# Branch merge and output projection computed in high and low parts, with the parts added on GpSimd

## The chip, the cores and the metric

One core of a Trainium2 chip runs the whole program. The metric is the device time of one execution in microseconds (us), the median of several runs. The engines are named as the profile names them: PE (TensorE matmul; PEld is its weight load), DVE (VectorE), ACT (ScalarE), POOL (GpSimd), SP (SyncE, which here issues nearly all transfers).

## What is computed

An encoder of two layers over 768 rows (a prompt of 256, a sample of 512), width 1024, in float32. Per layer four attention branches (A, B, C, X) give outputs `oa`, `ob`, `oc` (512 wide) and `ox` (256 wide); then come the lines that the change touches, and then 16 experts chosen by their top rows:

```python
merged = (gates[:, :, 0] * (oa @ wb[BR_A:BR_B])
          + gates[:, :, 1] * (ob @ wb[BR_B:BR_C])
          + gates[:, :, 2] * (oc @ wb[BR_C:BR_X])
          + gates[:, :, 3] * (ox @ wb[BR_X:]))
x = x + merged @ w_out[l]
x = x + expert_choice_moe(rms_norm(x, norm2_g[l]), w_router[l], w_gate_up[l], w_down[l])
```

## The kernel before

The program is written per engine, each with its instructions in a fixed order, and the engines wait for each other on counted signals (`Signal`; `at(l, k)` is the k-th event of layer l). A layer runs through these stages: norms and projections of the rows, the attention of A, B, C and X, the merge, the output projection with the second norm and the router between its tiles, the choice of rows, and the experts.

Most matrix products are already in three single-pass parts: `product3` (L1782) multiplies high by high, high by low and low by high, all of type float32r, into one bank. ACT makes a high part as a copy with rounding, DVE the low part as the difference of the raw value and the high part. The gate columns of `w_in` are multiplied like this between the attention's matmuls (`gate_part`, L1833 to L1848), and ACT and SP put them into `g_cols` in DRAM.

The merge is different: it multiplies plain float32. PE goes over 8 column tiles `c` of 128, within each over the 4 branches `b`, and within each over two groups of rows (512 and 256); a group is 4 matmuls in depth (2 for X) of the weights `wdir` with the attention outputs `oT` (L2016 to L2029). Four banks turn. DVE multiplies each bank by the gate (L1654, L1657) and, for the last three branches, adds it to `mT` (L1659). ACT takes the sigmoid of the gates `G` (L1178). SP loads `oT` after the last pair of heads, then `wdir` in pieces of 1792 KB, `G` in pieces of 1536 KB, the projection's weights `wout0`, `wout1`, and `X2`, the rows to be added to (L711 to L742). `wdir` lies in the memory of the gate weights, so its first piece waits until all of those are split (`load_branch(0, lo_made, NGEMM - 1)`), behind the last gate stores on the queue.

The output projection (`project`, L2032 to L2043) multiplies `mT` by `wout` in 12 groups of 8 matmuls of 512 columns, with the transposes and router matmuls of the tile before in between (`turn_h`, `route`). DVE adds the residual (L1665), norms, and picks the top rows (L1699 to L1703). Then POOL gathers the first expert's rows, PE transposes them, ACT and DVE split them, and the experts start. The first two pairs of expert weights (`EARLY`, L758) are loaded after the merge, the rest after the projection's last matmul.

Of the kernel before, what the change touches and what calls it, by code (L numbers as in the profile page):

```python
# [12 lines left out]
P = 128  # L13
# [11 lines left out]
NE = 16  # L25
# [23 lines left out]
EARLY = 2  # L49
TILES = (2, 3, 4, 5, 0, 1)  # L50
NSAMPLE = 4
# [128 lines left out]
def build(nc, x_in, mem_in, w, gains, tables, y_prompt, y_sample):  # L180
    ctx = ExitStack()
    with ctx:
# [20 lines left out]
        fgs = sb("fgs", [P, 2, 512])  # L203
        mkv = sb("mkv", [P, MT, 2 * 4 * HD])
# [72 lines left out]
        wdir = take("wdir", [P, 2, 2 * SLOT])  # L277
        wout0 = take("wout0", [P, KD, 512])
# [4 lines left out]
        wkvp = take("wkvp", [P, 2, 4 * HD])  # L283
        take = rows_region()
# [77 lines left out]
        oT = take("oT", [P, 14, NTOK])  # L362
        mT = take("mT", [P, KD, NTOK])
        wout1 = take("wout1", [P, KD, 512])
        gp = take("gp", [P, 2, NTOK])

# [102 lines left out]
        o_in = dma_sig("o_in", 1)  # L469
# [3 lines left out]
        br_in = [dma_sig(f"br_in{i}", 2) for i in range(2)]  # L473
# [4 lines left out]
        wo_in = [dma_sig(f"wo_in{i}", 1) for i in range(2)]  # L478
# [65 lines left out]
        def o_of(br, h, s):  # L544

            t0, nt = SEQS[s]
            r, c = slice(h % 2 * HD, (h % 2 + 1) * HD), slice(t0 * P, (t0 + nt) * P)
            if br.name == "X":
                return oT[r, 12 + h // 2, c]
            return (OSB if br.name in "AC" and h < 2 else OS)[r, c]  # L550
# [32 lines left out]
        def _(sp):  # L583
# [29 lines left out]
            for l in range(DEPTH):  # L613
# [97 lines left out]
                sp.dma_start(oT[:, 0:12, :], o_rows[:, :].rearrange("(k p) n -> p k n", p=P)).then_inc(o_in.sem, 16)  # L711
                for g in (14, 15):
                    for i in range(4):
                        store_gate(l, g, i)

                def load_branch(n, before, k0):

                    sp.wait_ge(before.sem, before.at(l, k0))
                    sp.dma_start(wdir[:, n % 2, 0:14 * CW].rearrange("p (k n) -> p k n", n=CW),
                                 kpn(lay(w["w_branch"], l)[:, :, n * CW:(n + 1) * CW])).then_inc(br_in[n % 2].sem, 16)  # L720

                def load_gates(c):
                    sp.wait_ge(br_ev.sem, br_ev.at(l, 8 * (c - 1) - 1))
                    sp.dma_start(G[:, c % 2], g_cols[:, :].rearrange("(b q p) n -> p b q n", p=P, q=KD)[:, :, c, :])\
                      .then_inc(g_in[c % 2].sem, 16)

                load_branch(0, lo_made, NGEMM - 1)
# [4 lines left out]
                load_branch(1, fg_mm, 4 * NGATE - 1)  # L732
                load_gates(1)
                for c, wo in enumerate((wout0, wout1)):
                    sp.wait_ge(o_ev.sem, o_ev.at(l, 55))
                    sp.dma_start(wo[:], kpn(lay(w["w_out"], l)[:, :, c * 512:(c + 1) * 512])).then_inc(wo_in[c].sem, 16)
# [20 lines left out]

                for i in range(EARLY):  # L758
                    load_pair_m(l * NE, i)
# [31 lines left out]
        def _(pool):  # L791
# [21 lines left out]
            for l in range(DEPTH):  # L813
# [3 lines left out]
                norm_p(l, BR["X"], 0)  # L817

# [48 lines left out]
        def _(act):  # L867
# [133 lines left out]

            def attend(l, br, it, halves):
# [27 lines left out]
                for u, (h, s, t, last) in enumerate(br.units):  # L1030
# [20 lines left out]
                    if br.name == "C" and it == 0 and u == 4:  # L1051
                        cx_roots(l, 3).then_inc(x_root.sem, 1)
                    for g, i in copies.get(u, []):
                        gate_copy(l, g, i)
# [26 lines left out]
            for l in range(DEPTH):  # L1081
# [93 lines left out]
                for c in range(KD):  # L1175
                    act.wait_ge(g_in[c % 2].sem, g_in[c % 2].at(l, c // 2))
                    for b in range(4):
                        act.activation(G[:, c % 2, b, :], G[:, c % 2, b, :], ACT.Sigmoid).then_inc(g_sig.sem, 1)  # L1178
# [31 lines left out]
                for h in range(2):  # L1210
                    part_copies(l, xs_t, h, 7, xsT_hi[:, 4 * h:4 * h + 4, :], xs_hi)
# [53 lines left out]
        def _(dve):  # L1265
# [198 lines left out]

            def attend(l, br, it, quarters):
# [69 lines left out]
                for u, (h, s, t, last) in enumerate(br.units):  # L1535
# [21 lines left out]
                    if br.name == "C" and it == 0:  # L1557
                        x_norm(l, u)
                    if last:
# [11 lines left out]
            for l in range(DEPTH):  # L1571
# [74 lines left out]
                for c in range(KD):  # L1646
                    for b in range(4):
                        dve.wait_ge(g_sig.sem, g_sig.at(l, 4 * c + b))
                        for h, (t0, n) in enumerate(((256, 512), (0, 256))):
                            q = 8 * c + 2 * b + h  # L1650
                            gate, acc = G[:, c % 2, b, t0:t0 + n], mT[:, c, t0:t0 + n]
# [556 lines left out]
```

## Time and profile before

| what | value |
|---|---|
| median of 3 runs | 3387.19 us (3383.3 to 3391.39) |
| the profiled execution | 3385.0 us, span 3383.2 us |
| PE busy | 3148.2 us, 93% of the span |
| DVE, ACT, POOL busy | 2092.1, 1881.2, 348.0 us |
| mean granted TensorE clock | 0.979 of full speed |

The span runs from the first to the last instruction. A line such as L2027 is a line of the kernel printed above. A float32 matmul shows as two records in the profile, a float32r matmul as one. The chain of waits is followed back from the last instruction; what lies on it sets the time.

### The profile page before, as it was taken

To read this page: it belongs to the slowest core of one execution; us is meant where nothing else is said; L and a number is where in the kernel's file an instruction comes from. 1 tells how busy PE (TensorE), PEld (TensorE's weight loads), DVE (VectorE), ACT (ScalarE), POOL (GpSimd) and SP (SyncE) were. 2 spreads that over 40 slices of the span, in tenths; PEclk is the share of its full clock that TensorE was granted. 3 is DMA by queue.
4 is the path that set the end of the run, shared out by engine and by line. 5 is a ranking of instruction groups with operands and counts; after the bars stand their busy time and mean duration, and the time that the engine had idled before them with its cause. 6 is when DMAs were issued, how large, how long until landed. Compare 5 with 4: busy or idle time off the path is not lost.

```text
span 3383.2 us, 45998 instructions
## 1 busy us (share of the span) xinstructions
PE 3148.2 (93%) x16388; PEld 2394.2 (71%) x16388; DVE 2092.1 (62%) x3016; ACT 1881.2 (56%) x3018; POOL 348.0 (10%) x476
## 2 busy tenths in 40 slices
PE   7999989899999799999999899998989988999997
PEld 7978777777555477777698787777765545777775
DVE  4565455664333788888846654556634347888886
ACT  4365555555213577777744755555541136777775
POOL 0021111111000111111000211101110001111110
PEclk9999999999999799999999999999999998999999
DMA  6112111222631799999941121111245237999996
GB/s 222 52 59 68 46 46 44 71 75 89 247 133 62 274 387 384 386 389 381 337 138 49 58 66 48 49 58 61 75 156 210 103 121 282 382 388 387 383 390 247
DMA packets 272987, 626.41 MB, mean 185 GB/s; under 512 B 14784, under 2 KB 100800, under 8 KB 272736
## 3 DMA queue, kind: packets, MB, share of 16 engines
q1 hardware_dynamic: 265360, 595.18, 47.7%
q0 software_dynamic: 7472, 29.17, 3.4%
q8 instruction: 96, 1.57, 0.2%
q14 instruction: 59, 0.48, 0.0%
HBM read 564.54 MB, written 66.06 MB: 186 GB/s over the span
## 4 chain that ended last, share of the span: by engine, by line
PE 80%; DVE 7%; ACT 5%; DMA 2%; issue 2%; POOL 1%; DVEq 1%; SPq 0%; ACTq 0%; POOLq 0%
PE bank L1785 13%; PE bank L1787 13%; PE bank L1786 13%; PE bank L1845 11%; PE bank L2027 9%; PE bank L2040 5%; PE bank L1877 3%; PE bank L1869 2%; PE bank L1896 2%; PE bank L1897 2%; PE bank L1984 1%; PE bank L2095 1%; PE bank L1986 1%; POOL PR L810 1%; ACT PH L1041 1%
## 5 line engine op out<-in xcount | busy, mean ns | idle before, releaser
L1282 DVE TENSOR_TENSOR mlo<-mraw,wlo 128x2048 fp32r<-128x2048 f32 x160 | 365.9, 2288 | 119.0 <-ACT wlo L895 116.8
L1786 PE MATMUL bank<-mlo,xsT_hi 128*96 128x512 f32 x1024 | 403.3, 394 | 0.0
L1845 PE MATMUL bank<-hT_lo,whi 128*128 128x512 f32 (+1 forms) x1024 | 381.9, 373 | 0.0
L1845 PE MATMUL bank<-hT_hi,whi 128*128 128x512 f32 (+1 forms) x1024 | 358.0, 350 | 12.1 <-ACT fgs L889 12.1
L895 ACT ACTIVATE wlo<-mraw 128x2048 fp32r<-128x2048 f32 x160 | 304.8, 1911 | 86.3 <-DMA mraw<-in_w_gate_up_dram 72.9
L1845 PE MATMUL bank<-hT_hi,wlo 128*128 128x512 f32 (+1 forms) x1024 | 350.5, 342 | 0.0
L810 POOL TENSOR_SCALAR PR<-PR,prec 128x256 f32<-128x256 f32 (+2 forms) x336 | 192.0, 572 | 1439.8 <-DVE prec L1543 1439.8
L2027 PE MATMUL bank<-oT,wdir 128*128 128x256 f32 (+1 forms) x896 | 293.1, 490 | 13.5 <-DMA wdir<-in_w_branch_dram 13.5
L1282 DVE TENSOR_TENSOR mlo<-mraw,whi 128x2048 fp32r<-128x2048 f32 x128 | 290.3, 2289 | 23.8 <-ACT whi L895 23.5
L1502 DVE TENSOR_REDUCE nmax<-bank 128x1 f32<-128x512 f32 (+1 forms) x240 | 134.6, 562 | 245.5 <-PE bank L1869 189.6
L1041 ACT ACTIVATE PH<-bank 128x256 fp32r<-128x256 f32 (+2 forms) x336 | 159.2, 474 | 220.5 <-PE bank L1897 126.7
L1785 PE MATMUL bank<-whi,hT_hi 128*128 128x256 f32 (+1 forms) x960 | 272.9, 284 | 0.1
L1786 PE MATMUL bank<-wlo,hT_hi 128*128 128x256 f32 (+1 forms) x960 | 270.9, 282 | 0.0
L1787 PE MATMUL bank<-whi,hT_lo 128*128 128x256 f32 (+1 forms) x960 | 270.8, 282 | 0.0
L2027 PEld LDWEIGHTS bank<-oT,wdir 128*128 128x128 f32 x896 | 171.5, 192 | 135.1 <-issue 105.5
L895 ACT ACTIVATE whi<-mraw 128x2048 fp32r<-128x2048 f32 x128 | 243.8, 1906 | 9.7 <-PE bank L1787 9.7
L1877 PE MATMUL bank<-ident,PR 128*128 128x128 f32 x960 | 166.8, 280 | 66.3 <-POOL PR L810 65.2
L1845 PEld LDWEIGHTS bank<-hT_lo,whi 128*128 128x128 f32 x1024 | 196.3, 192 | 44.0 <-issue 27.7
L1845 PEld LDWEIGHTS bank<-hT_hi,whi 128*128 128x128 f32 x1024 | 195.9, 191 | 41.8 <-ACT fgs L889 10.2
L1845 PEld LDWEIGHTS bank<-hT_hi,wlo 128*128 128x128 f32 x1024 | 196.7, 192 | 31.8 <-issue 14.2
L1786 PEld LDWEIGHTS bank<-mlo,xsT_hi 128*96 128x96 f32 x1024 | 166.5, 163 | 70.7
L1519 DVE TENSOR_TENSOR PL<-bank,PH 128x256 fp32r<-128x256 f32 (+2 forms) x336 | 177.7, 529 | 53.7 <-ACT PH L1041 53.0
(263 smaller groups left out, 7091.9 us busy)
## 6 DMA issues: line engine op xcount, KB each, us to landing
mraw<-in_w_gate_up_dram SPq DMA_DIRECT2D x128, 2048.0 KB, 11.9
mraw_d<-in_w_down_dram SPq DMA_DIRECT2D x96, 1024.0 KB, 16.9
wraw<-in_w_in_dram SPq DMA_DIRECT2D x50, 1024.0 KB, 5.8
mraw<-in_w_down_dram SPq DMA_DIRECT2D x32, 1024.0 KB, 17.0
G<-g_cols SPq DMA_DIRECT2D x16, 1536.0 KB, 6.5
g_cols<-fgs SPq DMA_DIRECT2D x64, 256.0 KB, 2.0
wdir<-in_w_branch_dram SPq DMA_DIRECT2D x8, 1792.0 KB, 11.3
oT<-o_rows SPq DMA_DIRECT2D x2, 4608.0 KB, 14.7
```

Of the source, the lines that this page charges most:

```text
L810: pool.tensor_scalar(PR[:, u % 3, 0:n], PR[:, u % 3, 0:n], prec[:, u % 4:u % 4 + 1], 1.0, ALU.mult, ALU.mult).then_inc(p_norm.sem, 1)
L895: act.activation(m_hi(pos), m_raw(pos), ACT.Copy).then_inc(hi_made.sem, 1)
L1041: act.activation(PH[:, k0:k0 + n, (t - t0) * P:(t - t0 + 1) * P], bank[3 + u % 2][:, 0:n * P].rearrange("p (k n) -> p k n", k=n), ACT.Copy)\
L1282: dve.tensor_tensor(m_lo(pos), m_raw(pos), m_hi(pos), ALU.subtract)\
L1519: dve.tensor_tensor(PL[:, k0:k0 + n, c], bank[3 + u % 2][:, 0:n * P].rearrange("p (k n) -> p k n", k=n), PH[:, k0:k0 + n, c], ALU.subtract ...
L1785: pe.matmul(out, lhs_hi, rhs_hi, start=first, stop=False)
L1786: pe.matmul(out, lhs_hi, rhs_lo, start=False, stop=False)
L1787: return pe.matmul(out, lhs_lo, rhs_hi, start=False, stop=last)
L1845: ins = pe.matmul(gate_banks[i % 2][:, 0:n], lhs, rhs, start=m == 0, stop=m == 3 * KD - 1)
L1877: ins = pe.transpose(bank[3 + u % 2][:, k * P:(k + 1) * P], PR[:, u % 3, k * P:(k + 1) * P], ident[:])
L2027: ins = pe.matmul(bank[q % 4][:, 0:n], wdir[:, c // 2 % 2, o:o + P], oT[:, 4 * b + k, t0:t0 + n], start=k == 0, stop=k == nk - 1)
L2040: ins = pe.matmul(bank[g % 4][:], mT[:, k, t * P:(t + 1) * P], (wout0, wout1)[c][:, k, :], start=k == 0, stop=k == KD - 1)
```

## The change

The merge goes by branch. PE runs 8 steps `p`: steps 0 and 1 are the two column halves of branch A, 2 and 3 of B, 4 and 5 of C, 6 and 7 of X (whose depth is half). A step takes 4 column tiles with two groups of rows each, in `product3`, over all 8 banks in turn. Attention outputs, branch weights, the merged rows and `w_out` are split into high (ACT) and low parts (DVE); the splits of the first weights and of branch A lie between the units of X's attention (`merge_high`, `merge_low`). X's own output stays in the chip (`oX`). DVE only multiplies by the gate: branch A straight into `mT`, the others into two buffers `gp`, which POOL adds to `mT` (24 adds of 128x768 a layer). The output projection takes high and low parts of `mT` and `w_out`. All four pairs of the first expert are loaded after the projection's last matmul, its down weights after its rows have come in, and its first two low parts are made before those of the gathered rows.

```diff
-        wdir = take("wdir", [P, 2, 2 * SLOT])
-        wout0 = take("wout0", [P, KD, 512])
+        mw_raw = take("mw_raw", [P, 6, SLOT])
...
+                load_o(0)
+                load_o(1)
+                sp.wait_ge(lo_made.sem, lo_made.at(l, NGEMM - 2))
+                load_branch(0)
...
-                for c in range(2, KD):
-                    load_gates(c)
-                    if c in (3, 5):
-                        load_branch(c // 2 + 1, br_mm, 8 * (c - 1) - 1)
+                for p in range(6):
+
+                    sp.wait_ge(br_mm.sem, br_mm.at(l, 8 * p + 7))
+                    if p + 2 < MWEIGHTS:
+                        load_branch(p + 2)
+                    if p == 1:
+                        load_o(2)
+                    if p == 5:
+                        load_out(2)
+                        load_out(3)
+
+                    sp.wait_ge(br_ev.sem, br_ev.at(l, 8 * p + 7))
+                    load_gates(p + 2)
...
-                for i in range(EARLY, PAIRS):
+                for i in range(PAIRS):
                     load_pair_m(l * NE, i)
+                sp.wait_ge(xs_in.sem, xs_in.at(l, 0))
...
+                for i in range(24):
+                    c = i % 8
+                    pool.wait_ge(br_ev.sem, br_ev.at(l, 17 + 2 * i))
+                    pool.tensor_tensor(mT[:, c, :], mT[:, c, :], gp[:, i % 2, :], ALU.add).then_inc(acc_made.sem, 1)
...
+                for p in range(MSTEPS):
+                    act.wait_ge(g_in[p % 2].sem, g_in[p % 2].at(l, p // 2))
+                    for i in range(4):
+                        act.activation(G[:, p % 2, i, :], G[:, p % 2, i, :], ACT.Sigmoid).then_inc(g_sig.sem, 1)
+                    if p + 1 < MWEIGHTS:
+                        weight_high(p + 1, br_mm if p else fg_mm)
...
+                for p in range(MSTEPS):
+                    for i in range(4):
+                        dve.wait_ge(g_sig.sem, g_sig.at(l, 4 * p + i))
+                        n0 = 4 * (p - 2) + i
                         for h, (t0, n) in enumerate(((256, 512), (0, 256))):
...
-                            if b == 0:
-                                dve.tensor_tensor(acc, gate, bank[q % 4][:, 0:n], ALU.mult).then_inc(br_ev.sem, 1)
-                            else:
-                                part = gp[:, b % 2, t0:t0 + n]
-                                dve.tensor_tensor(part, gate, bank[q % 4][:, 0:n], ALU.mult)
-                                dve.drain()
-                                dve.tensor_tensor(acc, acc, part, ALU.add).then_inc(br_ev.sem, 1)
+                            if p >= 2:
+                                dve.wait_ge(acc_made.sem, acc_made.at(l, n0 - 2))
+                            out = mT[:, 4 * p + i, t0:t0 + n] if p < 2 else gp[:, n0 % 2, t0:t0 + n]
+                            dve.tensor_tensor(out, G[:, p % 2, i, t0:t0 + n], bank[q % 8][:, 0:n], ALU.mult).then_inc(br_ev.sem, 1)
+                        if i == 0 and p + 1 < MWEIGHTS:
+                            weight_low(p + 1)
...
+                        if p == 7 and i < 3:
+                            merged_low(i)
+                for c in range(3, 4):
+                    merged_low(c)
+                for q in (2, 3):
+                    out_low(q)
+                    for c in range(2 * q, 2 * q + 2):
+                        merged_low(c)
...
+                for p in range(MSTEPS):
+                    b, w = p // 2, min(p, MWEIGHTS - 1)
+                    nk = 2 if b == 3 else 4
+                    pe.wait_ge(mw_lo.sem, mw_lo.at(l, 3 + w))
+                    pe.wait_ge(oc_lo.sem, oc_lo.at(l, 4 * b + nk - 1))
...
                     for k in range(k0, k1):
-                        ins = pe.matmul(bank[g % 4][:], mT[:, k, t * P:(t + 1) * P], (wout0, wout1)[c][:, k, :],
-                                        start=k == 0, stop=k == KD - 1)
+                        if g == 0:
+                            pe.wait_ge(mt_lo.sem, mt_lo.at(l, k))
+                        ins = product3(bank[g % 4][:], mT_hi[:, k, t], mT_lo[:, k, t], wo_hi(2 * c + k // 4, k % 4),
+                                       wo_lo(2 * c + k // 4)[:, k % 4, :], k == 0, k == KD - 1)
```

On DVE, the start of the merge of layer 0, before the change (`oT` is the last output of X's attention, then tile `c` = 0):

```order
944 L1511 TENSOR_TENSOR oT<-bank,oT 64x512
945 L1654 TENSOR_TENSOR mT<-G,bank 128x512
946 L1654 TENSOR_TENSOR mT<-G,bank 128x256
947 L1657 TENSOR_TENSOR gp<-G,bank 128x512
948 L1659 TENSOR_TENSOR mT<-mT,gp 128x512
949 L1657 TENSOR_TENSOR gp<-G,bank 128x256
950 L1659 TENSOR_TENSOR mT<-mT,gp 128x256
```

The same place after the change, up to the second tile of step 0 (`mw_r` are the parts of branch weights; `o_lo` the low parts of attention outputs):

```order
952 L1675 TENSOR_TENSOR oX<-bank,oX 64x512
953 L1840 TENSOR_TENSOR mT<-G,bank 128x512
954 L1840 TENSOR_TENSOR mT<-G,bank 128x256
955 L1815 TENSOR_TENSOR mw_r<-mw_raw,mw_r 128x2048
956 L1617 TENSOR_TENSOR o_lo_131<-o_raw_123,o_hi_125 128x768
957 L1840 TENSOR_TENSOR mT<-G,bank 128x512
```

The adds are gone from this queue, and the low parts of the next step's weights and of the next branch stand between the multiplies.

On ACT, from step 5 to the end of the merge after the change (`G` is the sigmoid, `mT_hi` the high parts of the merged rows, `wo_hi` those of the projection's weights):

```order
857 L1307 ACTIVATE G<-G 128x768 x4
858 L1285 ACTIVATE mw_r<-mw_raw 128x2048
859 L1089 ACTIVATE oX_hi<-oX 128x768 x2
860 L1293 ACTIVATE wo_hi_139<-mw_raw 128x2048
861 L1307 ACTIVATE G<-G 128x768 x4
862 L1302 ACTIVATE mT_hi<-mT 128x768 x2
863 L1307 ACTIVATE G<-G 128x768 x4
864 L1302 ACTIVATE mT_hi<-mT 128x768 x2
865 L1296 ACTIVATE wo_hi2a<-mw_raw 128x1024
866 L1296 ACTIVATE wo_hi2b<-mw_raw 128x1024
867 L1302 ACTIVATE mT_hi<-mT 128x768 x2
```

Where ACT had only sigmoids, the high parts of merged rows and of the second half of `w_out` now follow the last sigmoid.

## Rows read from the trace of the kernel before

**Rows 1.** The page's busy time: us, share of the span, instructions.

```profile
PE 3148.2 (93%) x16388; PEld 2394.2 (71%) x16388; DVE 2092.1 (62%) x3016; ACT 1881.2 (56%) x3018; POOL 348.0 (10%) x476
```

**Rows 2.** The page's chain that ended last, its shares by engine and line.

```profile
PE bank L1785 13%; PE bank L1787 13%; PE bank L1786 13%; PE bank L1845 11%; PE bank L2027 9%; PE bank L2040 5%; PE bank L1877 3%; PE bank L1869 2%; PE bank L1896 2%; PE bank L1897 2%; PE bank L1984 1%; PE bank L2095 1%; PE bank L1986 1%; POOL PR L810 1%; ACT PH L1041 1%
```

**Rows 3.** The chain around layer 0's merge: start us, us, what.

```profile
852.70 145.81 PE bank L2027 x444
...
1000.95 20.87 PE bank L2040 x48
```

**Rows 4.** Timeline of PE, each layer's first merge record: start, us, idle before.

```profile
852.70 1.22 PE L2027 MATMUL bank<-oT,wdir 128*128 128x512 f32 x1 [6.59 <-DMA wdir<-in_w_branch_dram]
...
2525.76 1.22 PE L2027 MATMUL bank<-oT,wdir 128*128 128x512 f32 x1 [6.92 <-DMA wdir<-in_w_branch_dram]
```

**Rows 5.** Stretches: PE, PEld, DVE, ACT, POOL busy (records), PE clock, DMA share, GB/s.

```profile
852.70:870.00 17.30, 17.30 (x48) 9.85 (x49) 4.52 (x8) 5.90 (x8) 0.00 (x0) 0.89 1.05 380
...
1180.00:1690.00 510.00, 509.28 (x2355) 359.08 (x2354) 441.38 (x269) 391.70 (x305) 65.79 (x55) 1.00 1.02 378
```

**Rows 6.** PE's groups, layer 0, 840 to 1100 us: records, busy, mean ns.

```profile
L2027 PE MATMUL bank<-oT,wdir 128*128 128x512 f32 x224 | 103.4, 602 | 6.6 <-DMA wdir<-in_w_branch_dram 6.6
L2040 PE MATMUL bank<-wout,mT 128*128 128x512 f32 x192 | 84.9, 595 | 1.6 <-DVE mT L1659 1.6
L2027 PE MATMUL bank<-oT,wdir 128*128 128x256 f32 x224 | 53.6, 379 | 0.0
```

**Rows 7.** Timeline of PE in A's attention: single-pass matmuls of 512 and 256 columns.

```profile
204.61 0.39 PE L1845 MATMUL bank<-hT_hi,wlo 128*128 128x512 f32 x1
204.84 0.28 PE L1845 MATMUL bank<-hT_hi,whi 128*128 128x256 f32 x1
204.96 0.38 PE L1877 MATMUL bank<-ident,PR 128*128 128x128 f32 x2
```

**Rows 8.** DVE's groups by shape: count, busy us, mean ns, idle before.

```profile
L1269 DVE TENSOR_TENSOR wlo<-wraw,whi 128x2048 fp32r<-128x2048 f32 x26 | 59.6, 2291 | 69.5 <-ACT whi L873 69.3
L1657 DVE TENSOR_TENSOR gp<-G,bank 128x512 f32<-128x512 f32 x48 | 33.0, 688 | 104.8 <-PE bank L2027 96.6 <-ACT G L1178 8.2
L1330 DVE TENSOR_TENSOR Z<-Z,stat_c 128x768 f32<-128x768 f32 x14 | 13.4, 958 | 1.3
```

**Rows 9.** ACT's groups by shape: count, busy us, mean ns, idle before.

```profile
L873 ACT ACTIVATE whi<-wraw 128x2048 fp32r<-128x2048 f32 x26 | 49.6, 1908 | 5.2 <-DMA wraw<-in_w_in_dram 5.0
L1178 ACT ACTIVATE G<-G 128x768 f32<-128x768 f32 x64 | 48.7, 831 | 203.6 <-DMA G<-g_cols 203.6
```

**Rows 10.** The page's transfers: KB each, median us from issue to landing.

```profile
wraw<-in_w_in_dram SPq DMA_DIRECT2D x50, 1024.0 KB, 5.8
G<-g_cols SPq DMA_DIRECT2D x16, 1536.0 KB, 6.5
```

**Rows 11.** POOL's groups by shape, its only tensor arithmetic: count, busy us, mean ns.

```profile
L810 POOL TENSOR_SCALAR PR<-PR,prec 128x512 f32<-128x512 f32 x128 | 89.4, 699 | 299.0 <-DVE prec L1543 299.0
L810 POOL TENSOR_SCALAR PR<-PR,prec 128x256 f32<-128x256 f32 x176 | 83.8, 478 | 1051.4 <-DVE prec L1543 1051.4
```

**Rows 12.** Timeline of POOL and of DVE around 504 us: start, us, instruction.

```profile
504.08 2.17 POOL L810 TENSOR_SCALAR PR<-PR,prec 128x512 f32<-128x512 f32 x2 [5.23 <-DVE prec L1543]
...
504.43 0.68 DVE L1276 TENSOR_TENSOR wlo<-wraw,whi 128x512 fp32r<-128x512 f32 x1
```

**Rows 13.** Timeline of DVE at the projection's last residual, layer 0.

```profile
1097.41 0.69 DVE L1665 TENSOR_TENSOR X<-X,bank 128x512 f32<-128x512 f32 x1 [1.16 <-PE bank L2040]
```

**Rows 14.** The chain at the first expert of layer 0: start us, us, what.

```profile
1118.81 7.26 DMA XS<-h_rows,ig
...
1126.12 0.92 PE bank L2095 x4
...
1127.58 0.57 DVE xsT_lo L1740
...
1132.62 0.74 PE bank L1785
```

More of the change, by code:

```diff
@@ L48 @@
 PAIRS = 4
-EARLY = 2
 TILES = (2, 3, 4, 5, 0, 1)
+MSTEPS = 8
+MWEIGHTS = 7
 NSAMPLE = 4
@@ L283, in build @@
         wkvp = take("wkvp", [P, 2, 4 * HD])
+        take = small()
+        wo_hi2a = take("wo_hi2a", [P, 2, 512], F32R)
         take = rows_region()
@@ L468, in build @@
         o_out = dma_sig("o_out", 12)
-        o_in = dma_sig("o_in", 1)
+        o_in = [dma_sig(f"o_in{i}", 1) for i in range(3)]
         fg_mm = sig("fg_mm", 4 * NGATE)
@@ L472, in build @@
         fg_out = [dma_sig(f"fg_out{i}", 2 * NGATE) for i in range(2)]
-        br_in = [dma_sig(f"br_in{i}", 2) for i in range(2)]
+        mw_in = [dma_sig(f"mw_in{i}", 4 - i) for i in range(2)]
+        mw_hi = sig("mw_hi", 3 + MWEIGHTS)
+        mw_lo = sig("mw_lo", 3 + MWEIGHTS)
+        oc_hi = sig("oc_hi", 14)
+        oc_lo = sig("oc_lo", 14)
         g_in = [dma_sig(f"g_in{i}", 4) for i in range(2)]
@@ L477, in build @@
         br_ev = sig("br_ev", 64)
-        wo_in = [dma_sig(f"wo_in{i}", 1) for i in range(2)]
+        acc_made = sig("acc_made", 24)
+        mt_hi = sig("mt_hi", KD)
+        mt_lo = sig("mt_lo", KD)
+        wo_in = [dma_sig(f"wo_in{i}", 1) for i in range(4)]
+        wo_hi_made = sig("wo_hi_made", 4)
+        wo_lo_made = sig("wo_lo_made", 4)
         x_in2 = dma_sig("x_in2", 1)
@@ L710, in _ @@
                 sp.wait_ge(prep_t.sem, prep_t.at(l, BR["X"].last_prep(0)))
[L711 to L720, printed above, removed]
@@ L1173, in _, with weight_high @@
                 attend(l, br, 0, [(1, 13, fg_mm, 4 * 13 + 3, 14)])
[L1175 to L1178, printed above, removed]
+                def weight_high(w, used):
+                    act.wait_ge(mw_in[w % 2].sem, mw_in[w % 2].at(l, w // 2))
+                    act.sem_inc(passed["act"], 1)
+                    act.wait_ge(used.sem, used.at(l, 4 * 15 + 3 if w == 1 else 8 * (w - 2) + 7))
+                    raw, hi, _ = m_weight(w)
+                    act.activation(hi, raw, ACT.Copy).then_inc(mw_hi.sem, 1)
@@ new lines, in out_high @@
+                def out_high(q):
+                    act.wait_ge(wo_in[q].sem, wo_in[q].at(l, 0))
+                    act.sem_inc(passed["act"], 1)
+                    act.wait_ge(br_mm.sem, br_mm.at(l, 31 if q < 2 else 47))
+                    if q < 2:
+                        ins = act.activation((wo_hi0, wo_hi1)[q][:], wo_raw(q), ACT.Copy)
+                    else:
+                        for h in range(2):
+                            ins = act.activation(((wo_hi2a, wo_hi2b), (wo_hi3a, wo_hi3b))[q - 2][h][:],
+                                                 wo_raw(q)[:, 2 * h:2 * h + 2, :], ACT.Copy)
+                    ins.then_inc(wo_hi_made.sem, 1)
@@ L1180, in mean_square @@
+                for c in range(2, 4):
+                    merged_high(c)
+                for q in (2, 3):
+                    out_high(q)
+                    for c in range(2 * q, 2 * q + 2):
+                        merged_high(c)
                 def mean_square(i):
@@ L1649, in _, with merged_low @@
+                def merged_low(c):
+                    dve.wait_ge(mt_hi.sem, mt_hi.at(l, c))
+                    dve.tensor_tensor(mT_lo[:, c, :], mT[:, c, :], mT_hi[:, c, :], ALU.subtract).then_inc(mt_lo.sem, 1)
+                for p in range(MSTEPS):
+                    for i in range(4):
+                        dve.wait_ge(g_sig.sem, g_sig.at(l, 4 * p + i))
+                        n0 = 4 * (p - 2) + i
                         for h, (t0, n) in enumerate(((256, 512), (0, 256))):
-                            q = 8 * c + 2 * b + h
@@ new lines, in _ @@
+                        if p == 5 and i < 2:
+                            o_low(l, 3, i)
+                        if p == 5 and i == 3:
+                            out_low(1)
+                        if p == 7 and i < 3:
+                            merged_low(i)
+                for c in range(3, 4):
+                    merged_low(c)
+                for q in (2, 3):
+                    out_low(q)
+                    for c in range(2 * q, 2 * q + 2):
+                        merged_low(c)
@@ L2025, in _ @@
                             for k in range(nk):
-                                o = (4 * b + k) * CW + c % 2 * P
-                                ins = pe.matmul(bank[q % 4][:, 0:n], wdir[:, c // 2 % 2, o:o + P],
-                                                oT[:, 4 * b + k, t0:t0 + n], start=k == 0, stop=k == nk - 1)
+                                ins = product3(bank[q % 8][:, 0:n], wh[:, k, c], wl[:, k, c], oh[:, k, t0:t0 + n],
+                                               ol[:, k, t0:t0 + n], k == 0, k == nk - 1)
@@ L2101, in turn_xs @@
                     turn_part(XS, h, 7, xs_t)
-                turn_xs(0, 0)
-                turn_xs(0, 1)
+                for h in range(2):
+                    pe.wait_ge(xs_in.sem, xs_in.at(l, 0))
+                    turn_part(XS, h, 7 - h, xs_t)
                 def expert(e, last):
```

180 lines of the change are left out of this document (144 added, 36 removed).

## The prediction, made before the changed kernel was run

> **What bounds the kernel now.** I read the busy times first: PE is busy 93% of the span [rows 1], so time is won only where PE has less to do or waits less. The shares of the chain say how much of it the changed lines are: L2027 (merge) 9% and L2040 (projection) 5% [rows 2]. Third, the chain around the merge: one unbroken PE piece of 145.81 us, then the projection's first 48 records in 20.87 us [rows 3]. Two records are one float32 matmul, so a product of 512 columns takes 20.87 / 24 = 0.87 us. The timeline shows PE idle ahead of each merge, 6.59 and 6.92 us, for the first `wdir` [rows 4]. So attention ends on PE at 846.1, the projection starts at 1000.95, and its first group of 8 ends 6.96 us later, at 1007.9: **161.8 us**, the stretch on which nearly everything below rests. Layer 1 runs the same instructions after the same wait. In the experts PE is busy 509.28 of 510 us [rows 5], started by their first operands: they move with what lies before and gain nothing of their own.
>
> **The change part by part, one layer.**
>
> *Products of the merge.* There are 224 records each at 512 and 256 columns [rows 6], hence 112 products of either size. Each becomes three single-pass matmuls. Their price is the distance between starts in A's attention, where the stationary operand also changes every time: 0.23 us after one of 512 columns, 0.12 after one of 256 [rows 7]. 112 x 3 x 0.23 + 112 x 3 x 0.12 = **117.6 us**. The recorded durations (602, 379 ns) overlap and are no price.
>
> *The wait ahead.* Weights and outputs of A are split inside X's attention, and SP loads them before the last gate stores; PE can go on at once. 6.6 us gone; it is inside the 161.8. The pieces of splitting are of the size of those that other units of attention carry already, so I cost them at nothing; if that cover fails, eight units late by 0.3 us are 2.4 us.
>
> *Loads and splits per step.* Steps 0 to 5 take PE 16 x (0.69 + 0.36) = 16.8 us, steps 6 and 7 half. When step p ends, its weight buffer is loaded with step p+2's: 5.8 us for 1024 KB [rows 10], ACT 1.9 [rows 9], DVE 2.3 [rows 8], 10 of 16.8 us; the gates behind it take 6.5 [rows 10] and four sigmoids of 0.83 [rows 9]. Covered. DVE stands at that low part meanwhile, with three tiles' multiplies behind it; eight banks let PE run on for a whole step, and DVE's multiplies (4 x (0.69 + 0.42) = 4.4 us a step) catch up. At step 0 the gates come some 6.5 us late, under the same cover. One place isn't covered: step 4 needs branch C's last low part, which DVE makes behind step 3's last multiplies: 0.42 + 0.96 [rows 8] = **1.4 us**.
>
> *The adds on POOL.* 24 of 128x768 with two inputs. Before, POOL works with one only: 0.478 us for 256 columns, 0.699 for 512 [rows 11], so 0.22 per 256 and 0.92 for 768. Lower bound 0.92. I take twice that, **1.84 us**, since two operands must be read; nothing in the rows sets the upper end, and I try 3.5. In steps 2 to 5 four adds (7.4 us) fit into 16.8, in steps 6 and 7 into 8.4 only just. The Trainium skill (GPSIMD Engine Reference, 3.1) speaks against this move: it prices a float32 add of 2048 columns at 4497 ns on GpSimd and 2293 on VectorE. Our 2291 ns agrees with the latter [rows 8]; by the former an add here would take about 1.69 us (an estimate by columns), and the sum would change by less than 1 us.
>
> *End of the merge.* Let E be the end of PE's last merge matmul. The gates of step 7 are asked for behind 2 MB of `w_out`, land about 11 us into the last 16.9, and leave DVE two tiles behind at E. DVE then has a pair of multiplies (1.1), six low parts of merged rows (6 x 0.96) and four halves of `w_out` (2 x 2.29): 11.4 us. The projection's first group takes each `mT_lo` as it comes, so it ends 0.7 behind the last, at E + 12.1. One add of 1.84 can get between, where DVE and POOL keep each other out: two POOL instructions of 0.70 took 2.17 together, 0.78 too much, over a DVE subtraction of 0.68 with two SBUF operands [rows 12]. So **E + 13.9**, against E + 5.5 without waits. The Trainium skill (SBUF — State Buffer, Who interferes with whom) says just this: a VectorE instruction with two SBUF inputs contends with a GpSimd one that reads SBUF, and the second fully blocks. By that the last add may also be kept out until DVE pauses, which is the second rival.
>
> *Sum to the end of the first group:* 117.6 + 1.4 + 13.9 = 132.9, so 161.8 - 132.9 = **28.9 us** won. While PE gets its operands drop by drop its clock may fall, as in the wait before the merge: behind that, 17.3 us ran at a granted 0.89, part at 1.2 GHz and the rest at 2.4 [rows 5]: 1.9 us lost. Before, the gap cost that too, and it is inside 161.8; now I charge **-1.9** for the end.
>
> *Rest of the projection.* 192 records [rows 6] are 96 products; 88 remain, each 0.87 - 0.69 = 0.18 less: 15.8. DVE picks top rows in its last part and now stands only 1.16 us ahead of the last residual [rows 13]; PE arrives 0.69 us sooner for each 4 products, three times from the picks' start, 2.1 us in all, so 0.9 is lost: **14.9 us**. The float32 router products stay.
>
> *First expert.* Both halves of the gathered rows are transposed at once, and two weight splits go ahead of them on DVE. Before, the rows landed at 1126.1 and the first product began at 1132.6 [rows 14]: 6.5 us. The first half alone goes from its transposes at 1126.12 through ACT to the end of DVE's part at 1128.15, 2.0 us; the second half's transposes add 0.9: 3.0. **3.5 us** won. The removed early loads cost nothing: from the projection's end (1097.4 [rows 13]) to the rows there are 28.7 us, and 8 MB at 380 GB/s need 22 [rows 5].
>
> Per layer 28.9 - 1.9 + 14.9 + 3.5 = 45.4; two layers **90.8 us**. The profiled execution took 3385.0, 2.2 below the median of the runs; from the median: 3387.2 - 90.8 = **3296 us**. 0.2%, about 7 us, is what a measurement can tell from no change.
>
> **Rivals.**
>
> *1. Cheaper ends.* POOL near 0.92 us and no exclusion: the first group ends at E + 12, the clock holds: 2 x 3.8 more, 3288. The floor, with no wait at all, is 2 x (1.4 + 8.4 + 1.9 + 0.9) = 25 below the forecast, 3271. For: single-input rows at 0.70. Against: the one long case of [rows 12].
>
> *2. POOL sets the end.* Exclusion with adds of 2.5 to 3.5 us: adds and DVE's two-operand work (low parts from step 2 on: 4 weights, 6 outputs, 4 quarters of `w_out`, 8 merged rows, 31.8 us) form one line. From step 2's first tile (38 us after the start): 38 + 31.8 + 24 x 2.5 = 130, inside the 132.9, but the adds come one by one behind the last steps and the group ends near E + 22; at 3.5, 38 + 31.8 + 84 = 154. That gives back 9 to 21 us a layer: 3313 to 3338. Kept-out adds at 1.84 alone give back 4 a layer: 3304.
>
> *3. Loads late.* If transfers run at 250 GB/s instead of 380, `X2` and the early pieces of `w_out` (in all 8 MB ahead of step 2's weights) land 11 us late, and the last gates 5: 16 a layer, 3328. Against: in the first 17 us of the old merge the queue moved 380 GB/s [rows 5].
>
> *4. Slower than before.* The line of rival 2 at the price at which all is lost: 38 + 31.8 + 24 T must exceed the 161.8 of before and the 14.9 + 3.5 won elsewhere, 180 us, so T = 4.6 us an add, five times the one-input price [rows 11]. At 5.5 us it is 22 a layer, 3430. PE would then wait at every `br_ev`. Nothing in the rows speaks for such a price; nothing shows the operation either.
>
> *5. Nothing happens*: merge and projection are on the chain with 14% [rows 2], so only if float32r matmuls were slower here than in [rows 7]. I see no reason.
>
> **How the numbers follow.** Forecast as worked out, with its ends of the tail (3283 to 3306): 0.62. Rival 1 beyond that: 0.08. Rival 2: 0.17. Rival 3: 0.07. Rival 4: 0.03. Rival 5: 0.02, and 0.01 for something unseen. The range takes the forecast, most of rival 1 and the nearer half of 2: 3281 to 3324. Faster 0.95, within 0.2% 0.02, slower 0.03.
>
> **What would show it.** Right: merge matmuls 0.23 and 0.12 apart; no PE idle before the first one; a merge of 118 to 121 us; PE waiting for `mT_lo` inside the first projection group, some 8 us in pieces; projection products 0.69 apart instead of 0.87; POOL adds near 1.8 us, some longer beside DVE's low parts; experts as before. Wrong: PE waiting for `br_ev` in steps 2 to 5 (POOL too slow, rivals 2 and 4), for `mw_lo` (loads, rival 3), a granted clock well under 1 within the merge, or X's attention longer than before.

## Result, and the profile after

The changed kernel takes 3304.73 us (median of 4 runs, 3303.0 to 3305.84) against 3386.31 us (4 runs, 3383.3 to 3391.39): a ratio of 0.9757, 95% interval 0.974 to 0.9774. That is 81.6 us won where 90.8 were forecast, inside the range and near its middle, 8.7 us above the predicted time. The page after, its busy times and the shares of its chain, which answer to [rows 1, 2]:

```profile
PE 3068.3 (93%) x17028; PEld 2471.2 (75%) x17028; DVE 2140.1 (65%) x3000; ACT 1955.4 (59%) x3094; POOL 449.0 (14%) x524
...
PE 79%; DVE 9%; ACT 5%; issue 2%; POOL 1%; DMA 1%; DVEq 1%; ACTq 0%; POOLq 0%; SPq 0%
```

(In the second line "issue" is time in which an engine waited for nothing that the profile shows, and a name ending in q is an engine's sequencer.) PE lost 80 us of work, POOL gained 101. Two of PE's groups of the merge in layer 0 (records, busy, mean ns) answer to [rows 6]:

```profile
L1983 PE MATMUL bank<-o_hi,mw_r 128*128 128x512 f32 x96 | 37.7, 393 | 1.4 <-issue 1.4
...
L1985 PE MATMUL bank<-o_hi,mw_r 128*128 128x256 f32 x96 | 27.2, 283 | 0.0
```

PE's timeline at the first branch matmul answers to [rows 4]:

```profile
850.20 0.40 PE L2095 MATMUL bank<-PL,VLX 128*128 128x512 f32 x1
850.43 0.39 PE L1983 MATMUL bank<-o_hi,mw_r 128*128 128x512 f32 x1
850.66 0.39 PE L1984 MATMUL bank<-o_lo,mw_r 128*128 128x512 f32 x1
```

The 6.6 us of idle time ahead of the merge are gone, and the products start 0.23 us apart. The one idle gap of 1.4 us in the groups is the predicted one at step 4, ahead of which DVE makes branch C's last low part:

```profile
917.82 0.95 DVE L1617 TENSOR_TENSOR o_lo<-o_raw,o_hi 128x768 fp32r<-128x768 f32 x1
...
918.88 0.47 PE L1983 MATMUL bank<-o_hi,mw_r 128*128 128x512 f32 x1 [1.43 <-issue]
```

Three stretches of layer 0 follow: the merge up to E (the end of its matmuls, here 969.21), the first projection group with its waits (it ends at 986.14; the stretch goes on to 987.40, where the clock is back at full), and the rest of the projection (columns as in [rows 5]):

```profile
850.43:969.21 118.78, 117.35 (x673) 103.32 (x672) 64.88 (x83) 51.90 (x57) 44.21 (x22) 1.00 0.61 226
969.21:987.40 18.19, 11.08 (x30) 7.23 (x29) 15.71 (x16) 6.38 (x8) 7.05 (x3) 0.62 0.08 29
987.40:1061.97 74.57, 73.58 (x386) 62.14 (x384) 25.74 (x57) 27.72 (x46) 0.00 (x0) 1.00 0.18 71
```

In the merge PE is busy 117.35 of 118.78 us at full clock; behind it PE works 11.08 of 18.19 us at a granted 0.62. DVE's timeline shows why, from the sigmoids of the last gates to the last low part, with POOL's last four adds under it and, last, an add with no subtraction of DVE's beside it:

```profile
965.11 1.02 DVE L1840 TENSOR_TENSOR gp<-G,bank 128x512 f32<-128x512 f32 x2 [2.35 <-ACT G L1307]
966.05 0.95 DVE L1828 TENSOR_TENSOR mT_lo<-mT,mT_hi 128x768 fp32r<-128x768 f32 x1
966.91 1.01 DVE L1840 TENSOR_TENSOR gp<-G,bank 128x512 f32<-128x512 f32 x2
967.84 1.69 DVE L1828 TENSOR_TENSOR mT_lo<-mT,mT_hi 128x768 fp32r<-128x768 f32 x1
...
974.50 2.84 DVE L1823 TENSOR_TENSOR mw_r<-mw_raw,wo_hi2a 128x1024 fp32r<-128x1024 f32 x1
977.27 1.21 DVE L1823 TENSOR_TENSOR mw_r<-mw_raw,wo_hi2b 128x1024 fp32r<-128x1024 f32 x1
...
982.41 1.81 DVE L1828 TENSOR_TENSOR mT_lo<-mT,mT_hi 128x768 fp32r<-128x768 f32 x2
...
966.21 10.05 POOL L898 TENSOR_TENSOR mT<-mT,gp 128x768 f32<-128x768 f32 x4 [0.98 <-DVE gp L1840]
...
937.06 1.83 POOL L898 TENSOR_TENSOR mT<-mT,gp 128x768 f32<-128x768 f32 x1 [2.09 <-DVE gp L1840]
```

From 965.11 to 984.2 DVE doesn't pause once. The same low part takes 0.95 us alone and 1.69 beside an add, half a weight piece 1.21 and 2.84, and four adds take 10.05 us, 2.5 each, where an add alone takes 1.83 to 1.86. The lengths are those of whole instructions kept out: POOL's last add ends at 976.26, and the half piece begun at 974.50 ends 1.08 us behind it.

The other place is the first expert. POOL's row-number copy and its gather, DVE's moved low parts and the landing of the rows as the chain has it (8.26 us after the issue began), layer 0 after the change, and then copy and gather before it (there the rows landed after 7.26 us [rows 14]):

```profile
1082.66 1.95 POOL L902 COPY ig<-idxT 96x1 uint32<-96x1 uint32 x1 [106.40 <-DVEq L1935]
1085.52 2.12 POOL L905 DMA_INDIRECT XS<-h_rows,ig  x1 [0.92 <-POOL ig L902]
...
1082.27 4.49 DVE L1431 TENSOR_TENSOR mlo<-mraw,whi 128x2048 fp32r<-128x2048 f32 x2
...
1085.52 8.26 DMA XS<-h_rows,ig
```

```profile
1117.71 0.18 POOL L821 COPY ig<-idxT 96x1 uint32<-96x1 uint32 x1 [275.29 <-DVEq L1736]
1118.81 1.01 POOL L824 DMA_INDIRECT XS<-h_rows,ig  x1 [0.92 <-POOL ig L821]
```

A copy of 96 numbers has become ten times longer: it began 0.39 us behind the start of DVE's first moved low part (`lo_moe`, L1431; two of them, 2.29 us each) and ends at 1084.61, 0.05 us behind that part.

Where the 80.2 us between the two spans come from, in us won (layer 0, layer 1):

| stretch | predicted a layer | measured |
|---|---|---|
| end of attention to end of the first projection group | 27.0 | 26.1, 26.4 |
| rest of the projection | 14.9 | 13.7, 14.2 |
| last residual to the first expert's first matmul | 3.5 | 0.4, 1.4 |
| all else | 0 | -2.1 in both together |

The last line is 4.3 us lost ahead of layer 0's merge and 2.2 won elsewhere. The 4.3 can't be put down to the change. The code ahead of layer 0's first merge is the same in the changed kernel and in all runs below, and yet the first merge matmul lies anywhere from 847.75 to 853.24 us in their profiles. X's attention, where the change put splits, is as long as before but for 0.1 us: from its first multiply on POOL to its last 58.01 us before (783.94 to 841.95) and 58.13 after (788.29 to 846.43), in layer 1 58.01 and 58.15. So a whole run says less here than the distance between two events of one trace, and I read both.

### The profile page after: what moved, and what is told of

The parts are those of the page before. It is cut to its first block, busy times and chain, and to the rows that moved or that the text cites. A ratio compares the mean times of both kernels' runs of the same rounds, so it can differ in the third digit from the quotient of the medians.

```text
span 3303.0 us, 47435 instructions
## 1 busy us (share of the span) xinstructions
PE 3068.3 (93%) x17028; PEld 2471.2 (75%) x17028; DVE 2140.1 (65%) x3000; ACT 1955.4 (59%) x3094; POOL 449.0 (14%) x524
## 4 chain that ended last, share of the span: by engine, by line
PE 79%; DVE 9%; ACT 5%; issue 2%; POOL 1%; DMA 1%; DVEq 1%; ACTq 0%; POOLq 0%; SPq 0%
PE bank L1983 17%; PE bank L1985 17%; PE bank L1984 17%; PE bank L2043 12%; PE bank L2075 3%; PE bank L2067 2%; PE bank L2094 2%; PE bank L2095 2%; PE bank L2182 1%; PE bank L2298 1%; PE bank L2184 1%; POOL PR L886 1%; ACT PH L1143 1%; DVE PL L1683 1%; PE bank L2064 1%
## 5 line engine op out<-in xcount | busy, mean ns | idle before, releaser
L1431 DVE TENSOR_TENSOR mlo<-mraw,wlo 128x2048 fp32r<-128x2048 f32 x160 | 366.2, 2289 | 112.6 <-ACT wlo L976 109.6
L1431 DVE TENSOR_TENSOR mlo<-mraw,whi 128x2048 fp32r<-128x2048 f32 x128 | 290.2, 2288 | 26.9 <-ACT whi L976 26.7
L2043 PEld LDWEIGHTS bank<-hT_hi,wlo 128*128 128x128 f32 x1024 | 197.5, 193 | 32.2 <-issue 14.3
L1983 PE MATMUL bank<-whi,xsT_hi 128*96 128x512 f32 x512 | 203.5, 398 | 2.7 <-DVE xsT_lo L1939 2.7
L1983 PE MATMUL bank<-wlo,xsT_hi 128*96 128x512 f32 x512 | 204.0, 399 | 0.2 <-DVE mlo L1431 0.2
```

The costliest lines, as they stand in the source:

```text
L1431: dve.tensor_tensor(m_lo(pos), m_raw(pos), m_hi(pos), ALU.subtract)\
L1983: pe.matmul(out, lhs_hi, rhs_hi, start=first, stop=False)
L2043: ins = pe.matmul(gate_banks[i % 2][:, 0:n], lhs, rhs, start=m == 0, stop=m == 3 * KD - 1)
```

## Experiments

Each is the changed kernel with the edit shown. "The tail" is the time from E to the first projection group's end (E+16.9 and, in layer 1, E+16.7).

**Is it the moved low parts that hold the gather?** First edit, DVE waits for the copy:

```diff
+                dve.wait_ge(ig_ok.sem, ig_ok.at(l, 0))
                 lo_moe(l, 0, 0)
                 lo_moe(l, 0, 1)
```

> Compared with the changed kernel (3304.7 us). VectorE waits, ahead of the first expert's first two low parts, until GpSimd's 96x1 copy of the row numbers is done. Theory 1 (the moved low parts, two operands in SBUF each, hold the copy): the copy falls from 1.95 to about 0.2 us, the gather is issued 1.8 us earlier and the first expert's first matmul comes 1.8 us earlier in each layer, 1.8 to 2.8 if the gather's landing (8.3 us after its issue, 7.3 in the kernel before) shrinks too: 3299 to 3301 us, 0.975 of before or just under. Theory 2 (the gather waits in the DMA engines behind the four pair loads that now all start late): the copy shrinks, but the landing takes so much longer, and the time stays at 3304 to 3305.

3303.41 us (ratio 0.9751, 0.9736 to 0.9766), between the two forecasts. POOL, layer 0:

```profile
1081.03 0.18 POOL L902 COPY ig<-idxT 96x1 uint32<-96x1 uint32 x1 [106.29 <-DVEq L1935]
1082.13 2.29 POOL L905 DMA_INDIRECT XS<-h_rows,ig  x1 [0.92 <-POOL ig L902]
```

The copy is back at 0.18 us, so the low parts did hold it. But from the copy's start to the first matmul 13.0 us are left of 14.1 in layer 0 and 13.1 of 13.9 in layer 1, not 12.3: the rows now land 9.0 us after the issue.

Second edit, the low parts behind the rows again, as before the change:

```diff
-                lo_moe(l, 0, 0)
-                lo_moe(l, 0, 1)
                 for h in range(2):
                     ...
-                lo_moe(l, 0, 2)
+                for pos in range(AHEAD):
+                    lo_moe(l, 0, pos)
```

> The first expert's three low parts are put back behind the low parts of the gathered rows, as before the change; all else as changed. Theory 1 (low parts hold the copy): copy 0.2 us, gather issued 1.8 us earlier, but from the turns of the gathered rows to the first matmul 6.5 us again instead of 2.9: 0.8 to 1.8 us a layer slower than the changed kernel, 3306 to 3308. Theory 2 (the gather waits for the pair loads, whatever VectorE does): 3.6 us a layer slower, 3312.

3304.42 us (0.9753, 0.9738 to 0.9768), less than either forecast. POOL, and the landing in the chain:

```profile
1082.20 0.18 POOL L902 COPY ig<-idxT 96x1 uint32<-96x1 uint32 x1 [106.28 <-DVEq L1935]
1083.30 1.01 POOL L905 DMA_INDIRECT XS<-h_rows,ig  x1 [0.92 <-POOL ig L902]
...
1083.30 7.69 DMA XS<-h_rows,ig
```

With DVE at rest the issue takes 1.01 us, as before the change, and the rows land after 7.7 us, although the same pair loads run. The matmul comes 13.8 us after the copy: putting the low parts ahead or behind is worth nothing, because what is won behind the rows (3.6 us) is lost ahead of them.

Third edit, DVE waits for a signal that POOL gives behind the gather (`pool.sem_inc(gathered.sem, 1)` after `gather(0, 0)`):

> VectorE's first two low parts of the first expert wait until GpSimd has also issued the gather (in the run that waited for the copy alone the issue still lasted 2.29 us and the rows landed 9.0 us after its start; with the low parts behind the rows 1.01 and 7.7 us). Theory (the low parts hold GpSimd's whole way to the gather, the copy and the making of the descriptors): copy 0.2, issue 1.0 us, landing 7.7 us, and from the copy's start to the first expert's first matmul 11.7 us instead of 14.1 (changed kernel) and 13.0 (wait for the copy alone): 2.3 us a layer, 3300 us. Rival (1.3 us of the landing belongs to the pair loads that share the DMA engines): 13.0 us again, 3302 to 3303.

The edit did not do what its text says:

```profile
1081.00 4.49 DVE L1433 TENSOR_TENSOR mlo<-mraw,whi 128x2048 fp32r<-128x2048 f32 x2 [1.42 <-POOLq L918]
...
1081.19 2.99 POOL L906 DMA_INDIRECT XS<-h_rows,ig  x1 [0.92 <-POOL ig L903]
```

DVE was released 0.19 us before the gather's record begins, the issue then took 2.99 us and the rows landed 9.7 us after it began. 13.75 us to the matmul; 3306.76 us, scattered from 3301.99 to 3311.13 (0.9768, 0.9755 to 0.9781). As a miss it still gives a row: issues of 1.01, 2.12, 2.29 and 2.99 us go with landings of 7.7, 8.3, 9.0 and 9.7. In the three long ones the issue ends 0.88 or 0.89 us behind the end of a low part (here 1084.18 and 1083.29), so it too waits for a whole instruction. The landings alone are weaker evidence: before the change, in layer 1, an issue of 0.99 us went with a landing after 8.2. Fourth edit, the signal comes from a second tiny copy, which POOL can only run once the gather is issued:

```diff
                 gather(0, 0)
+                pool.tensor_copy(isc[:], idxT[:, 0:1]).then_inc(gathered.sem, 1)
...
+                dve.wait_ge(gathered.sem, gathered.at(l, 0))
                 lo_moe(l, 0, 0)
```

> In the run before, the signal behind the gather came 0.9 us after the copy, ahead of the issue's own record, so the low parts still lay beside the issue (2.99 us, rows landed 9.8 us after it began). Now VectorE waits for a second 96x1 copy on GpSimd, which can run only when the descriptors are made. Theory (the low parts hold the making of the descriptors as they hold the copy): issue 1.0 us, landing 7.7 us, from the copy's start to the first expert's first matmul 11.7 to 12 us instead of 13.9 to 14.1: 2 us a layer, 3299 to 3302 us. Rival (the landing depends on the pair loads): issue 1.0 us but landing 9 to 10 us, 13 us or more to the matmul: 3303 to 3306.

```profile
1085.64 0.18 POOL L903 COPY ig<-idxT 96x1 uint32<-96x1 uint32 x1 [106.47 <-DVEq L1937]
1086.74 1.01 POOL L906 DMA_INDIRECT XS<-h_rows,ig  x1 [0.92 <-POOL ig L903]
1087.76 0.20 POOL L918 COPY isc<-idxT 96x1 uint32<-96x1 uint32 x1
```

Landing after 7.8 us and 11.84 and 11.54 us from copy to matmul: 2.2 and 2.3 us won, at the place and of the size that the theory says; the rival (pair loads) falls. The time, 3302.28 us (0.9749, 0.9733 to 0.9766), can't show 4.5 us by itself.

**What makes the tail?** First, POOL's adds cut to one column:

```diff
-  pool.tensor_tensor(mT[:, c, :], mT[:, c, :], gp[:, i % 2, :], ALU.add)
+  pool.tensor_tensor(mT[:, c, 0:1], mT[:, c, 0:1], gp[:, i % 2, 0:1], ALU.add)
```

> GpSimd's 24 adds per layer are cut to one column of 768 (128x1 instead of 128x768), so the parts of branches B, C and X are left out of the merged rows but for that column; every wait and signal stays. Theory (while GpSimd adds, VectorE's two-operand low parts stand still): in the tail the low parts fall from 1.67-1.69 to 0.95 us and from 2.84 to 1.21 us, VectorE's unbroken run from 19.1 to 15.2 us, the waits for the adds of step 6 go, and the first projection group ends at E+12 to E+13 instead of E+16.9: 4 to 5 us a layer, 3294 to 3298 us. Rival (the last gates' load and VectorE's own work set the end, the adds only lie beside it): low parts keep their lengths, E+16 to E+17, 3303 to 3305.

3300.53 us (0.9744, 0.9729 to 0.9759). DVE's groups between 936 and 990 us, here and in the changed kernel:

```profile
L1828 DVE TENSOR_TENSOR mT_lo<-mT,mT_hi 128x768 fp32r<-128x768 f32 x8 | 7.5, 952 | 0.0
...
L1823 DVE TENSOR_TENSOR mw_r<-mw_raw,wo_hi2a 128x1024 fp32r<-128x1024 f32 x1 | 1.2, 1220 | 0.0
```

```profile
L1828 DVE TENSOR_TENSOR mT_lo<-mT,mT_hi 128x768 fp32r<-128x768 f32 x8 | 9.6, 1220 | 0.0
...
L1823 DVE TENSOR_TENSOR mw_r<-mw_raw,wo_hi2a 128x1024 fp32r<-128x1024 f32 x1 | 2.8, 2843 | 0.0
```

DVE's unbroken run falls from 19.1 to 15.3 us in both layers: 3.8 us of it are DVE standing still for POOL. The group ends at E+13.1 in layer 0, 3.8 us sooner, and at E+13.9 in layer 1, 2.7 sooner: there its last matmuls now start 0.43 us apart, at the lower of the clock's two levels (1.2 GHz), and it ends 1.9 us behind the last low part instead of 0.8. The time lies between the two forecasts, and its interval overlaps that of the changed kernel; what decides is the trace. Second, the adds on DVE instead:

```diff
+                        if p >= 2:
+                            dve.drain()
+                            acc = mT[:, n0 % 8, :]
+                            dve.tensor_tensor(acc, acc, gp[:, n0 % 2, :], ALU.add).then_inc(acc_made.sem, 1)
```

> The 24 adds of each layer run on VectorE (drain, then add, behind each pair of products) instead of GpSimd. Theory (while a two-operand low part runs on VectorE, GpSimd's add stands still and the other way round, so an add on GpSimd costs VectorE nearly as much as its own): the tail of 19.1 us loses the 3.9 us of stretched low parts and gains four adds of about 1.05 us: the first projection group ends at E+16 to E+18, low parts take 0.95 and 1.21 us everywhere, and the time is 3302 to 3308. Rival A (GpSimd really takes work off VectorE): VectorE gains 24 adds of 1.05 us in the merge, has no slack in the steps that also split rows, and PE waits for it: 5 to 10 us a layer, 3315 to 3325. Rival B (GpSimd's chain alone sets the end): the end comes 3 to 4 us a layer sooner, 3297.

3308.23 us (0.9765, 0.975 to 0.9781), an interval that contains the changed kernel's ratio. Low parts take 0.95 and 1.22 us, an add 0.96, and DVE's run in the tail 19.5 us: in the tail the adds cost DVE as much on POOL as on DVE. The merge to E grew by 1.1 us; rival A, with 5 to 10, falls. So moving the adds to POOL is worth about 3.5 us of the 81.6, which the two times can't tell from nothing (the traces, from the first merge matmul to the first expert's, have 2.7 and 1.2), though POOL was idle.

Third, the last gates loaded ahead of the last two weight pieces:

```diff
-                    if p == 5:
-                        load_out(2)
-                        load_out(3)
                     sp.wait_ge(br_ev.sem, br_ev.at(l, 8 * p + 7))
                     load_gates(p + 2)
+                    if p == 5:
+                        load_out(2)
+                        load_out(3)
```

> SP starts the last gate load ahead of the two last pieces of the output projection's weights instead of behind them. Theory (the last gates, landing 10.1 us after issue and 1.7 us after ACT asks for them, start VectorE's unbroken run of 19 us that ends the merge): the load lands in 6 to 7 us, ACT's last sigmoids come 1.5 to 2 us earlier, and the first projection group ends at E+15.0 to E+15.4 instead of E+16.9 (E is the end of the merge's matmuls): 3300 to 3302 us. Rival (GpSimd's adds set the end: the four of step 6 run back to back to 965.2, the four of step 7 follow 1 us later): the sigmoids come earlier but the products wait for the adds to free their buffers, at most 1 us a layer is won: 3303 to 3305.

3305.1 us (0.9761, 0.9745 to 0.9776): as the rival has it. The last sigmoids start at 962.34 instead of 964.23 and DVE's run at 963.49, held until then by POOL's adds (0.79 us of waiting a pair); the group ends 0.9 and 0.7 us sooner after E, and layer 1 gives 0.8 back in the projection, whose first 20 us run at a clock of 0.96 instead of 1.00. Fourth, this with DVE's work reordered:

```diff
-                for c in range(3, 4):
-                    merged_low(c)
+                for c in range(3, 8):
+                    merged_low(c)
                 for q in (2, 3):
                     out_low(q)
-                    for c in range(2 * q, 2 * q + 2):
-                        merged_low(c)
...
-                            pe.wait_ge(wo_lo_made.sem, wo_lo_made.at(l, 2 * c + 1))
+                            pe.wait_ge(wo_lo_made.sem, wo_lo_made.at(l, 2 * c))
...
+                        if i == 0 and k == 4:
+                            pe.wait_ge(wo_lo_made.sem, wo_lo_made.at(l, 2 * c + 1))
```

> At the end of the merge VectorE makes the low parts of the last four merged tiles ahead of those of the two last weight pieces, which only the second projection group reads; PE's second group waits for each piece as it needs it; the last gates are loaded first. Theory (VectorE's unbroken run sets the end, and its order decides what PE gets when): the first projection group ends at E+10.5 to E+12.5 instead of E+16.9, but the second then waits for its weights and ends 1.5 to 3 us earlier than in the changed kernel: 3299 to 3302 us. Rival (what the end wins goes back as lower clock in the projection, as in the run with the gates first, which won 0.8 us a layer there and kept none): 3303 to 3305.

3293.86 us (0.9724, 0.9711 to 0.9738), below the changed kernel's interval and 5 us better than the theory's best. The stretch from 969 to 984 and the 22 us behind it, first in this kernel and then in the changed one (E at 967.82 and 969.21):

```profile
969.00:984.00 15.00, 12.18 (x39) 8.39 (x38) 13.51 (x13) 4.29 (x5) 4.95 (x2) 0.77 0.11 36
984.00:1006.00 22.00, 22.00 (x115) 18.62 (x114) 6.23 (x11) 9.07 (x15) 0.00 (x0) 1.00 0.22 89
```

```profile
969.00:984.00 15.00, 7.89 (x23) 4.79 (x22) 15.00 (x15) 6.59 (x8) 7.26 (x3) 0.66 0.09 36
984.00:1006.00 22.00, 22.00 (x103) 18.33 (x102) 4.31 (x9) 6.74 (x10) 0.00 (x0) 0.92 0.12 48
```

DVE does the same work, stretched as before (the lows of the merged rows 6.76 us for five), but the first group ends at E+11.9 and the second follows without a pause: its end moves from E+23 to E+17.5. I had let the second wait for its weights; they came in time, piece by piece. From E to the last residual 5.5 and 4.7 us are won. Last, this together with the wait for the gather: first with the signal that came too early, then with the second copy.

> Both of the two: low parts of the first expert behind the gather's issue, and the order of the end. If the two places are independent the gains add: 4.6 us from the first and 3 to 5 from the second, 3295 to 3298 us; if the clock takes the end's gain back, 3299 to 3301.

3297.63 us (0.9732, 0.9719 to 0.9745): 13.7 and 13.5 us from copy to matmul, so the end's gain alone.

> The same wait together with the order of the end that gave 3293.9 us. If the two places are independent, 2 us a layer below that: 3288 to 3292 us; if not, 3293 to 3296.

3291.78 us (0.9721, 0.9704 to 0.9737). The trace has both gains, 87.3 us from E to the last residual and 11.69 and 11.66 us from the copy to the matmul. By time it can't be told from the order of the end alone (3293.86 us); it beats the changed kernel by 0.4%.

**Does PE set the pace of the merge?** One of the three products is left out:

```diff
-   ins = product3(bank[q % 8][:, 0:n], wh[:, k, c], wl[:, k, c], oh[:, k, t0:t0 + n], ol[:, k, t0:t0 + n], ...)
+   pe.matmul(bank[q % 8][:, 0:n], wh[:, k, c], oh[:, k, t0:t0 + n], start=k == 0, stop=False)
+   ins = pe.matmul(bank[q % 8][:, 0:n], wl[:, k, c], oh[:, k, t0:t0 + n], start=False, stop=k == nk - 1)
```

> The merge leaves out one of its three products (the low part of the rows by the high part of the weights); every split, load, wait and add stays. Theory (PE sets the pace of the merge's eight steps, the other engines' work is covered with a margin): from the first to the last branch matmul 118.8 us becomes 78.4 us of products plus stalls where a step of 11.2 us no longer hides a weight's load, its high and its low part (5.1, 1.9 and 2.3 us) or the rows of the third branch: 80 to 92 us, and 3225 to 3250 us in all. Rival (the splits and GpSimd's adds already set the pace and PE fills the gaps): over 105 us, over 3275 us.

3286.66 us (one run). The merge takes 103.4 us to E in layer 0 and 103.5 in layer 1, between the two forecasts and nearer to the rival's, and the time is well over the theory's: both sides hold in part. The stretch in layer 0:

```profile
850.54:953.98 103.44, 86.07 (x449) 74.04 (x447) 60.74 (x78) 48.27 (x53) 43.80 (x20) 0.92 0.70 259
```

Two of PE's waits between 845 and 960 us (waiting for what: us in total, times, longest):

```profile
PE bank L2228 <- DVE mw_r L1815: 8.4, 2, 5.4
PE bank L2228 <- issue: 6.7, 2, 6.0
```

PE does set the pace in the changed kernel (117.35 of 118.78 us), but with a third of its work gone only 15.4 of 39.2 us come back: 17.4 us are idle, half of it for weights' low parts and 6.0 ahead of step 4, where branch C's last low part ends at 913.93 and PE starts at 914.03, and the granted clock of 0.92 takes 7.7 more (86.07 us of matmuls where 78.4 were due). So PE sets the pace of the merge as it is, but not of one that is shorter by a third.

## Why the prediction was right, and where it missed

- *Products* and *the wait ahead*: as forecast. The merge to E takes 118.78 us in both layers, 117.6 + 1.4 = 119.0 forecast; PE starts 0.23 us after attention.
- *Loads and splits per step*: covered but for step 4's low part, 1.43 us against 1.4. The run with two products shows where that cover ends. X's attention, with the first splits, is 0.1 us longer.
- *The adds on POOL*: 1.84 us predicted, 1.83 to 1.86 measured alone (937.06 us and others). The estimate from the Trainium skill (GPSIMD Engine Reference, 3.1), 1.69 us, is 8% low.
- *End of the merge*: the mechanism was right (DVE's low parts set the end, PE gets `mT_lo` drop by drop and its clock falls), its exclusion mis-sized. PE waits 7.1 us in pieces for `mT_lo`, some 8 forecast. I charged one kept-out add, 1.84 us. The runs show 3.8, of which 3.1 lie behind E: four of DVE's subtractions beside an add are stretched, the low parts of three tiles of merged rows by 0.7 us each and half a weight piece by 1.6. Two more terms of that sum are off. It leaves two tiles at E and counts one pair of multiplies, where the trace has two (969.46 and 971.98), 1.0 us more; and the clock, charged with 1.9, costs layer 0 only 1.2 (the group ends 1.9 behind the last low part instead of 0.7). E+13.9 and 1.9 for the clock were 15.8; it is 16.9 and 16.7. This was the second rival's milder form, "kept-out adds at 1.84 alone", priced there at 4 us a layer more; that its 3304 is what was measured is partly chance, since the tail gave back only 1.1. The Trainium skill (SBUF — State Buffer, Who interferes with whom) had the rule, and these runs agree with it both ways: adds go from 1.84 to 2.5 us and more, low parts from 0.95 to 1.69, and each waits for the end of a whole instruction of the other.
- *Rest of the projection*: 14.9 forecast, 13.7 and 14.2 measured; DVE stands 1.14 us behind PE at layer 0's last residual where I had 0.9. Another 0.6 of layer 0 is the clock: the first three matmuls of the second group, from 986.14 to 987.38, still start 0.43 us apart, at 1.2 GHz. Some 0.4 us a layer stay open.
- *First expert*: **the step that failed**, 3.5 forecast, 0.4 and 1.4 measured, over half of what is missing. Its own reasoning held (from the turned rows to the first matmul 6.5 us became 2.9), but I put two DVE instructions of 2.29 us with two SBUF operands ahead of the rows and did not ask who works at that moment: POOL, on the copy and the gather that bring these rows. I had priced exclusion at the merge, where I looked for it, and not where the change created it anew. With the low parts behind a second copy (the run of 3302.28 us) the stretch from the last residual to that matmul takes 32.5 and 32.2 us instead of 34.8 and 34.9, so 2.7 and 4.1 are won against before (35.2 and 36.3): 6.8 in both layers, where 7.0 were forecast.
- *The sum*: 90.8 forecast; the three stretches measure 82.3 in all. 5.1 of the 8.5 missing are the first expert, 1.5 the end of the merge, 1.9 the rest of the projection.

## What to carry to other kernels

An idle GpSimd is no free engine for arithmetic on SBUF while VectorE runs subtractions of two SBUF operands: here 24 adds a layer on it were worth about 3.5 us in all. Count both as one line, and at the end of a stage order that line by who waits for what. The cheapest gain here, 10 us from E to the last residuals, was an order: first the low parts that the next matmul needs, the others behind. And when an instruction moves ahead of a wait, look at what every other engine does inside that wait.

## What was unexpected of the hardware

- Even POOL's smallest work is held: a copy of 96x1 took 1.95 instead of 0.18 us beside a low part of 2.29 us, which it waited out, and the issue of a gather 2.1 to 3.0 instead of 1.0, with the rows landing up to 2 us later after it.
- A semaphore that POOL raises behind a gather came before the gather's issue was over; a tiny copy behind it came after.
- Gaps on PE cost more than their length. With two products, 17.4 us of gaps brought 7.7 us of slower matmuls at the granted clock of 0.92.
